# Delta rule in a two-block layer: the decay sums of a head group as two products on rounded operands, and its three sets of chunk products moved into one half

## The reference, cut to what matters

```python
CHUNK, DN_HEADS, DN_HEAD_DIM = 64, 16, 128

def gated_delta_chunked(q, k, v, g, beta):
    gc = jnp.cumsum(g, axis=-1)                       # g: log decay of each token
    causal = idx[:, None] >= idx[None, :]
    strict = idx[:, None] > idx[None, :]
    decay = jnp.exp(jnp.where(causal, gc[..., :, None] - gc[..., None, :], -jnp.inf))
    kb = k * beta[..., None]
    A = jnp.einsum('bhnid,bhnjd->bhnij', kb, k) * decay * strict
    T = lax.linalg.triangular_solve(eye + A, ...)     # inverse of I + A
    u = jnp.einsum('bhnij,bhnjd->bhnid', T, v * beta[..., None])
    w = jnp.einsum('bhnij,bhnjd->bhnid', T, kb * jnp.exp(gc)[..., None])
    qk = jnp.einsum('bhnid,bhnjd->bhnij', q, k) * decay
    ...                                               # then a scan over the chunks
```

## Time and profile before

| what | value |
|---|---|
| median of 3 runs | 2372.1 us (2371.13 to 2373.28) |
| span of the profiled execution | 2369.2 us |
| time of that execution itself | not listed apart; the median lies 2.9 us above the span |
| TensorE busy | 2341.7 us (99%) |
| VectorE busy | 1627.3 us (69%) |
| ScalarE busy | 1175.1 us (50%) |
| GpSimd busy | 235.1 us (10%) |
| granted TensorE clock in 40 slices | 9 tenths or more in each |

### The profile page before, as it was taken

The page is one execution under the profiler, slowest core; times in us unless marked ns, Lnnn a source line. Parts: engine busy times, 40 slices in busy tenths (PEclk is TensorE's granted clock), DMA queues, the critical chain, the costliest instruction groups (busy, mean ns, idle before and its releaser), DMA issues.

```text
span 2369.2 us, 35126 instructions
## 1 busy us (share of the span) xinstructions
PE 2341.7 (99%) x13692; PEld 1923.2 (81%) x13692; DVE 1627.3 (69%) x2147; ACT 1175.1 (50%) x1554; POOL 235.1 (10%) x410
## 2 busy tenths in 40 slices
PE   8999999999999999999999999999999999999998
PEld 7888888777777777788888888888888888888887
DVE  5899999868787878656665756666666544555565
ACT  5555555566454545444564654545353444443443
POOL 3000001112121213011000101000010000000100
PEclk9999999999999999999999999999999999999999
DMA  7566667766555557588655557676776755675673
GB/s 252 188 216 200 203 202 232 223 198 224 180 192 177 193 179 269 171 280 287 219 195 195 188 177 235 225 234 230 231 236 224 245 191 189 228 259 191 223 251 124
DMA packets 239247, 506.87 MB, mean 214 GB/s; under 512 B 15065, under 2 KB 15938, under 8 KB 238210
## 3 DMA queue, kind: packets, MB, share of 16 engines
q1 hardware_dynamic: 214898, 418.57, 53.6%
q0 software_dynamic: 24208, 86.31, 11.2%
HBM read 464.45 MB, written 40.39 MB: 213 GB/s over the span
## 4 chain that ended last, share of the span: by engine, by line
PE 64%; DMA 2%; DVE 1%; ACT 0%; issue 0%; POOL 0%; DVEq 0%; ACTq 0%
PE acc L2599 57%; PE acc L2619 2%; DMA delta_branch_spill<-ol 1%; PE acc L2634 1%; PE aux L2661 1%; PE aux L3107 0%; PE aux L2806 0%; DMA r1l<-delta_branch_spill 0%; PE aux L3112 0%; PE aux L3012 0%; PE aux L2647 0%; PE acc L3012 0%; PE aux L2912 0%; DMA r1l<-conv_branch_spill 0%; PE aux L2899 0%
## 5 line engine op out<-in xcount | busy, mean ns | idle before, releaser
L1639 DVE TENSOR_TENSOR w_lo<-raw,w_hi 128x1024 fp32r<-128x1024 f32 x790 | 963.3, 1223 | 659.7 <-ACT w_hi L960 648.1
L960 ACT CAST w_hi<-raw 128x1024 fp32r<-128x1024 f32 x790 | 824.5, 1049 | 987.9 <-PE acc L2599 947.1
L2599 PE MATMUL acc<-w_hi,r1h 128*128 128x512 f32 x1828 | 722.7, 395 | 2.8 <-DVE w_lo L1639 2.0
L2599 PE MATMUL acc<-w_lo,r1h 128*128 128x512 f32 x1828 | 709.3, 388 | 0.0
L2599 PE MATMUL acc<-w_hi,r1l 128*128 128x512 f32 x1828 | 708.9, 388 | 0.0
L2599 PE MATMUL acc<-w_hi,r2h 128*128 128x512 f32 x1208 | 472.2, 391 | 0.3 <-DVE r2l L1733 0.3
L2599 PE MATMUL acc<-w_hi,r2l 128*128 128x512 f32 x1208 | 470.2, 389 | 0.0
L2599 PE MATMUL acc<-w_lo,r2h 128*128 128x512 f32 x1208 | 470.1, 389 | 0.0
L2599 PEld LDWEIGHTS acc<-w_hi,r1h 128*128 128x128 f32 x1828 | 343.4, 188 | 81.4 <-DVE w_lo L1639 6.1
L2599 PEld LDWEIGHTS acc<-w_hi,r1l 128*128 128x128 f32 x1828 | 343.5, 188 | 72.0
L2599 PEld LDWEIGHTS acc<-w_lo,r1h 128*128 128x128 f32 x1828 | 343.7, 188 | 66.0
(11 more groups left out here) (507 smaller groups left out, 1609.3 us busy)
## 6 DMA issues: line engine op xcount, KB each, us to landing
raw<-in_w_in SPq DMA_DIRECT2D x263, 1024.0 KB, 5.1
raw<-in_w_out SPq DMA_DIRECT2D x32, 1024.0 KB, 5.1
raw<-in_w_br_b SPq DMA_DIRECT2D x16, 1024.0 KB, 6.4
raw<-in_w_br_a SPq DMA_DIRECT2D x16, 1024.0 KB, 6.7
raw<-in_w_ple_gate SPq DMA_DIRECT2D x16, 1024.0 KB, 5.1
raw<-in_w_o_mla SPq DMA_DIRECT2D x16, 1024.0 KB, 5.1
raw<-in_w_o_conv SPq DMA_DIRECT2D x16, 1024.0 KB, 5.0
raw<-in_w_q_b SPq DMA_DIRECT2D x8, 1024.0 KB, 5.0
```

The lines of the kernel that those rows point to most:

```text
L960: nc.scalar.copy(w_hi[:, h % HL, 0:n], raw[:, k % RAW, x * HALF:x * HALF + n]).then_inc(hi_ready, 1)
L1639: V.tensor_tensor(w_lo[:, h % HL, 0:n], raw[:, k % RAW, x * HALF:x * HALF + n], w_hi[:, h % HL, 0:n].bitcast(F32), ALU.subtract).then_inc( ...
L2599: ins = T.matmul(acc[:, s, x, 0:n], a[:, kt0 + k, xs_], w[:, h % HL, at], start=start and k == 0 and m == 0, stop=stop and k == kts - 1 an ...
```

## The change

It replaces the float32 sum over the masked logs by two matmuls on rounded operands: ScalarE rounds `gm` to `gmh` at half 30, VectorE subtracts to `gml` at half 31, and TensorE adds the product with `gmh` and that with `gml` in bank 0. The mask `strict_lo` gets a rounded copy, once. `gm` is written at half 29 instead of 31. On TensorE the sum, the k by k products and the q by k products all stand behind half 0, in this order; the exponential on ScalarE moves from half 2 to half 1.

```diff
--- before.py
+++ after.py
@@ -292,6 +292,7 @@
         ident = sb("ident", [P, P])
         tri_incl = sb("tri_incl", [P, P])
         strict_lo = sb("strict_lo", [P, P])
+        strict_r = sb("strict_r", [P, P], F32R)
         same = sb("same", [P, P])
         half_ones = sb("half_ones", [P, 2, P])
         lvl = sb("lvl", [P, LEVELS - 1, BLK])
@@ -384,6 +385,7 @@
             otok, qdT = s1("otok", [P, TT, GH, P]), s1("qdT", [P, GH, TOK])
             decT, xs, bf, uinv, tinv = [s1(n, [P, TT, GH, SEQ_CHUNK]) for n in ("decT", "xs", "bf", "uinv", "tinv")]
             qkT = s1("qkT", [P, TT, GH, SEQ_CHUNK])
+            gmh, gml = [s1(n, [P, TT, GH, SEQ_CHUNK], F32R) for n in ("gmh", "gml")]
             state = s1("state", [P, GH, DK])
             oh, ol = s1("oh", [P, GH, TOK], F32R), s1("ol", [P, GH, TOK], F32R)
 
@@ -1081,6 +1083,9 @@
                     glu_gate(used(PH["GLU0"], 7), freed(PH["GLU0"], 0))
                 if hl == 1:
                     decays_softplus()
+                if hl == 4:
+                    act.wait_ge(sem("mask_ready"), MASK_TRI)
+                    nc.scalar.copy(strict_r[:], strict_lo[:]).then_inc(sem("strict_ready"), 1)
                 if hl == 6:
                     decays_exp()
                 if hl == 7:
@@ -1210,6 +1215,11 @@
                                 c.inc(ins)
                         sig(ins, "tap0_ready", n + 1)
 
+            def decay_hi(i):
+
+                act.wait_ge(sem("gm_ready"), i + 1)
+                nc.scalar.copy(gmh[:].rearrange("p t h i -> p (t h i)"), gm[:].rearrange("p t h i -> p (t h i)")).then_inc(sem("gm_hi"), 1)
+
             def z_tanh(ph, i, first=False):
                 if not first:
                     act.wait_ge(sem("o_gated"), i)
@@ -1226,7 +1236,7 @@
                         "w_ready", dv(2, n + 1))
 
             def delta(hl, dv):
-                if hl == 2:
+                if hl == 1:
                     act.wait_ge(sem("decay_done"), dv(1, 1))
                     sig(A(decT[:].rearrange("p t h i -> p (t h i)"), X[:, 0], ACT.Exp), "decT_ready", dv(1, 1))
                 if hl == 9:
@@ -1322,6 +1332,8 @@
                 for step in range(4 * NJ):
                     if hl == LN_VALUE[step]:
                         ln_value(step)
+                if hl == 30:
+                    decay_hi(0)
             z_tanh(ph, 0, True)
             act.wait_ge(sem("uT_out"), 32 * NJ)
             c.restart()
@@ -1333,6 +1345,8 @@
                     ahead(ph, hl, i)
                     delta(hl, dv)
                     own(ph, hl, i, False)
+                    if hl == 30:
+                        decay_hi(i)
                 z_tanh(ph, i)
                 c.restart()
 
@@ -1975,9 +1989,12 @@
                         dve.wait_ge(sem("tok_ready"), i * 2 + (n + 1))
                         sig(V.tensor_reduce(col(8 + n), cy[:].rearrange("p a n -> p (a n)").rearrange("p (m d) -> p m d", d=DK), AX.X, ALU.add),
                             "qk_square", i * 2 + (n + 1))
-                if hl == 31:
+                if hl == 29:
                     dve.wait_ge(sem("decay_cols"), i + 1)
                     sig(V.tensor_tensor(th(gm), rep(tri_c[:], TC2), over(col(7), SEQ_CHUNK), ALU.mult), "gm_ready", i + 1)
+                if hl == 31:
+                    dve.wait_ge(sem("gm_hi"), i + 1)
+                    sig(V.tensor_tensor(th(gml), th(gm), th(gmh).bitcast(F32), ALU.subtract), "gm_lo", i + 1)
 
             def z_silu(ph, i):
                 dve.wait_ge(sem("tanh_ready"), i + (TANH_Z + 1))
@@ -2833,14 +2850,16 @@
             def delta(hl, dv, own_tr=0):
 
                 if hl == 0:
-                    pe.wait_ge(sem("tok_ready"), dv(2, 2))
-                    per_chunk(2, columns_of(kT), columns_of(kT)).then_inc(sem("B_done"), 1)
-                if hl == 1:
                     if dv(2, 0):
                         pe.wait_ge(sem("oT_hi"), dv(2, 0))
                         pe.wait_ge(sem("oT_lo"), dv(2, 0))
-                    pe.wait_ge(sem("gm_ready"), dv(1, 1))
-                    T.matmul(X[:, 0], strict_lo[:], gm[:].rearrange("p t h i -> p (t h i)"), start=True, stop=True).then_inc(sem("decay_done"), 1)
+                    else:
+                        pe.wait_ge(sem("strict_ready"), 1)
+                    pe.wait_ge(sem("gm_lo"), dv(1, 1))
+                    T.matmul(X[:, 0], strict_r[:], gmh[:].rearrange("p t h i -> p (t h i)"), start=True, stop=False)
+                    T.matmul(X[:, 0], strict_r[:], gml[:].rearrange("p t h i -> p (t h i)"), start=False, stop=True).then_inc(sem("decay_done"), 1)
+                    pe.wait_ge(sem("tok_ready"), dv(2, 2))
+                    per_chunk(2, columns_of(kT), columns_of(kT)).then_inc(sem("B_done"), 1)
                     per_chunk(1, columns_of(kT), columns_of(qT), True).then_inc(sem("qk_done"), 1)
                 for l in range(LEVELS):
                     if hl == 5 + 2 * l:
```

## The result

The changed kernel has a median of 2378.6 us over seven runs (2375.3 to 2383.8), the kernel before 2372.1 over seven (2370.6 to 2376.0). The ratio is 1.0026 with a 95% interval of 1.0017 to 1.0035: **slower by 4 to 8 us**. In a second set, of eleven runs made with the experiments, it was 1.0022 (1.0013 to 1.0031): 2377.3 against 2371.5. The forecast was 2376.1 us, in a range from 2373.0 to 2378.3: the second median lies in it, the first 0.3 us above its end. Both intervals hold 0.2%, so the change lies at the border of the forecast's "within 0.2%" and "slower".

A forecast was written before the change was run, and what follows sets the result against it. TensorE, busy 99%, was taken to bound the kernel, with VectorE full ahead of `xs`. Three loop iterations (3.15 us) and YB (0.8) add 3.95 us to 2372.1, giving 2376.1 us, range 2373.0 to 2378.3.

The forecast's parts named there:

- within 0.2%: Forecast outcome for the whole kernel: time within 0.2% of the kernel before, chance 0.71.
- slower: Forecast outcome for the whole kernel: slower by over 0.2%, above 2376.8 us, chance 0.27.
- The bound and the narrow place: TensorE waits for nobody; VectorE, full from half 3 to `xs`, finishes 0.12 us before TensorE's product with `xs` starts.
- The price on TensorE: TensorE's own row over halves 0 and 1: -0.61 us in each of four places, from +1.54 - 2.04 - 0.11.
- The stand: TensorE's wait for `xs` at half 6, behind VectorE's late work: some 1.65 us.
- The net per iteration: Loop iterations i = 1, 2, 3: TensorE's product with `xs` comes 1.05 us later each, 3.15 for the loop.
- In YB +0.8: YB's product with `xs` moves from 947.31 to about 948.1, +0.8 us; TensorE's own gain is worth nothing there.
- Sum of the mechanism: Loss at half 6 over the three loop iterations and YB: 3.15 + 0.8 = +3.95 us.
- rival 2: At half 0 the pair waits for a late subtraction on VectorE: +4.0 us on top, 2380.1 us, chance 0.07.
- The small work: ScalarE's rounding at half 30 (0.59 us) and VectorE's subtraction at half 31 (0.69 us) are covered and cost nothing.
- Rival 3: The pair runs at the float32 rate, 1.92 instead of 0.46 us, +1.46 four times: 2382 us, chance 0.02.
- Rival 1: Only TensorE's sum counts: VectorE makes up its lateness, no wait at half 6; 2370.0 us, chance 0.10.

## Why the prediction was right, and where not

**The bound and the narrow place: right.** In the kernel before TensorE waited for nobody, and the slack at `xs` was only 0.12 us. The run with the keys moved shows that it was VectorE's row between halves 2 and 6.

**The price on TensorE: -0.61, measured -0.75.** The pair at 0.24 us each was right. The step from k by k to q by k products was taken as 1.08 and is 0.98, since no wide matmul stands between the two sets, and that from q by k to half 1 as 1.08 and is 1.04. By the four passes that the Trainium skill, page FP8 and Floating Point Precision, section TensorE Precision Notes, gives true FP32, the estimate would have been -0.56, further off. The trace agrees with four passes: the two halves of the old matmul start 0.43 us apart, near two steps of 0.23.

**The stand: 1.65, measured 1.66.** The net per iteration of 1.05 was 0.98, as half 1 starts 1.42 us later and not 1.54. In YB +0.8 was +0.65 in both profiles. The shift of VectorE, predicted as 1.08 us, was 1.04, and its 10.47 us from half 3 to `xs` held. Sum of the mechanism: 3.6 us instead of 3.95.

**The step that failed** is the sentence that behind the stand VectorE and TensorE are both 1.05 late and stand to each other as before, and with it the sum, which priced a stand of 1.65 us at its length alone. Behind a stand of this length the clock may fall, at 1.6 us each time: twice in one profile of the changed kernel, once in the other. The mechanism with one or two falls is 5.2 or 6.8 us, and the medians moved by 6.5 and 5.8; the parts far from the change move by 1 to 2 us from profile to profile. The sign of it was in the trace of before, at 474 us. That the medians still lie near the end of the range and not far beyond it is in part luck: its upper half was there for rival 2, a late subtraction, which did not come, and held the falls of the clock instead. The same clock explains part of the changed kernel's wider spread of 8.5 us in its first set, against 5.4 before; that the number of falls makes it was not shown run by run.

**The small work: right.** ScalarE's cast took 0.62 us and VectorE's subtraction 0.69. The pair never waited for `gm_lo`, in the first group neither, where 0.16 us was left. Rival 2 did not come. Rival 3 neither.

**Rival 1 did not come**: the wait at half 6 was there in all four places. The Trainium skill, page Perfetto Trace Analysis, section Identifying the Most-Contended Engine, would have one relieve the engine of the highest occupancy, and judges TensorE among others by the busy share of its weight loads, 81% here and also above VectorE's 69%. The trace agrees that TensorE bounds the kernel, but not that relieving it is enough: it was relieved, and the end came later, by an engine at 69% that was full for 10 us in each of four places.

## What to carry to other kernels

Before work is gathered at one point of the bounding engine's row, follow what that point's end releases, engine by engine, to where the bounding engine takes the result back, and write down the least slack on the way; a share of busy time over the whole kernel does not show it. Where a moved block delays a release, look for work of the late engine that can move into the wait which the move makes. And price a stand of TensorE at more than its length once it is longer than those after which the clock held.

## What the runs showed of the hardware that was not expected

The granted clock fell to 1.2 GHz behind stands as short as 1.66 us (5 of 11), for 7 or 8 matmuls of 512 columns at 0.43 us instead of 0.23, starting 1.0 to 1.7 us after work went on; behind the stand of 2.14 us at 471 to 474 us it did in 13 of 14 profiles, and behind stands of 1.54 us or less between 573 and 1060 us in none. Two sets of float32 matmuls of 64 columns stand 0.98 us apart, where a set followed by the 512-column projection takes 1.04 to 1.08; the step into a set is 0.09 us longer than usual and the first step of the projection behind one 0.1, whether rounded or float32 matmuls stand ahead of the set. And 21 more matmuls in the program brought a stand of 2.3 us at one place far from them, with no releaser in the profile.
